# A z tile in pieces of the front stage, and a substitution moved from GpSimd to VectorE

## The reference, cut to what matters

```
proj = rmsnorm(x) @ w_in                 # 1024 -> xr, yr (512 each), qkv (1536), z (512), gates
h    = rglru(conv(xr)); out_rg = gelu(yr) * h          # gates: sigmoid(xc @ w_a), sigmoid(xc @ w_i)
q,k,v = silu(conv(qkv)); q, k normalized per head
per chunk of tokens and head: A = I + strict_lower(beta * (k k^T) * decay)
u, w = A^-1 [beta v, beta k e^g];  qk = (q k^T) * decay
S, o: recurrence over chunks from qk, u, w
out_gdn = rmsnorm(o) * silu(z)
x = x + [out_rg, out_gdn] @ w_out;  x = x + (silu(hf w_gate) * (hf w_up)) @ w_down
```

## Time and profile before

| | before |
|---|---|
| three runs | 1474.85, 1476.22, 1478.69 us; median 1476.22 |
| the profiled execution | 1474.63 us, span 1472.8 us |
| granted clock, mean | 0.985 |
| PE busy | 1416.4 us, 96% |
| DVE, ACT, POOL busy | 625.5, 373.3, 158.6 us |
| input block | 0 to 328.7 us |
| front stage | 328.7 to 400.8 us |
| sample states, two z tiles | 400.8 to 456 us |
| chunk loop begins | 462.1 us |

### The profile page before, as it was taken

One profiled execution on the slowest core, in us unless ns is written; L12 is line 12 of the kernel. 1 busy time (PEld: TensorE's weight loads), 2 busy tenths in 40 slices (PEclk: granted clock), 3 DMA queues, 4 the chain that ended last, 5 costly groups with the idle time before them and its releaser, 6 DMA issues.

```text
span 1472.8 us, 20785 instructions
## 1 busy us (share of the span) xinstructions
PE 1416.4 (96%) x8140; PEld 1299.6 (88%) x8140; DVE 625.5 (42%) x929; ACT 373.3 (25%) x612; POOL 158.6 (11%) x251
## 2 busy tenths in 40 slices
PE   6999999998898999999999999999999999999997
PEld 6888899997786899889898989898989898989895
DVE  6365455533352666643424242424242424242416
ACT  5345544332251222122020202020202020202012
POOL 3000000105474222210000000000000000000001
PEclk9999999997999999999999999999999999999999
DMA  6102211243544444327110101010101010100003
GB/s 224 62 18 75 75 69 74 100 145 133 194 173 126 140 129 126 123 99 283 54 58 29 57 28 57 28 57 28 57 28 57 28 57 28 57 28 28 0 0 121
DMA packets 66810, 119.93 MB, mean 81 GB/s; under 512 B 14672, under 2 KB 40208, under 8 KB 66768
## 3 DMA queue, kind: packets, MB, share of 16 engines
q1 hardware_dynamic: 66768, 119.36, 23.7%
HBM read 90.00 MB, written 29.34 MB: 81 GB/s over the span
## 4 chain that ended last, share of the span: by engine, by line
PE 46%; issue 2%; DMA 2%; ACT 2%; DVE 1%; SPq 0%; POOL 0%; ACTq 0%; DVEq 0%; POOLq 0%
PE bank L92 16%; PE bank L94 15%; PE bank L93 15%; ACT gu_hi L2060 1%; DMA gu_first_raw<-in_w_up 1%; DMA out_y<-y_out 1%; DVE acc L2146 0%; DVE y_out L2110 0%; DVE hf L2122 0%; ACT y_out L2096 0%; SPq L1987 0%; ACT gu_first_hi L2060 0%; SPq L1983 0%; POOL fstat L2161 0%; ACTq L81 0%
## 5 line engine op out<-in xcount | busy, mean ns | idle before, releaser
L92 PE MATMUL bank<-ht_hi,w_hi 128*128 128x364 f32 (+1 forms) x576 | 191.5, 332 | 0.0
L94 PE MATMUL bank<-ht_hi,w_lo 128*128 128x364 f32 (+1 forms) x576 | 189.9, 330 | 0.0
L93 PE MATMUL bank<-ht_lo,w_hi 128*128 128x364 f32 (+1 forms) x576 | 189.8, 330 | 0.0
L2122 DVE TENSOR_TENSOR hf<-sg,bank 128x364 f32<-128x364 f32 (+1 forms) x66 | 35.1, 532 | 338.6 <-PE bank L94 335.3
L92 PE MATMUL bank<-ht_hi,gu_hi 128*128 128x364 f32 (+1 forms) x528 | 173.2, 328 | 0.9 <-DVE hf L2122 0.9
L92 PE MATMUL bank<-ht_hi,gu_first_hi 128*128 128x364 f32 (+1 forms) x528 | 173.6, 329 | 0.5 <-PEq L930 0.5
L94 PE MATMUL bank<-ht_hi,gu_first_lo 128*128 128x364 f32 (+1 forms) x528 | 173.5, 329 | 0.0
L93 PE MATMUL bank<-ht_lo,gu_first_hi 128*128 128x364 f32 (+1 forms) x528 | 173.4, 328 | 0.0
L93 PE MATMUL bank<-ht_lo,gu_hi 128*128 128x364 f32 (+1 forms) x528 | 173.1, 328 | 0.0
L94 PE MATMUL bank<-ht_hi,gu_lo 128*128 128x364 f32 (+1 forms) x528 | 173.1, 328 | 0.0
L2146 DVE TENSOR_TENSOR acc<-acc,bank 128x512 f32<-128x512 f32 (+1 forms) x198 | 132.3, 685 | 90.3 <-PE bank L94 90.3
(11 more groups left out here) (297 smaller groups left out, 2213.5 us busy)
## 6 DMA issues: line engine op xcount, KB each, us to landing
w_raw<-in_w_in SPq DMA_DIRECT2D x24, 512.0 KB, 4.4
dn_raw<-in_w_down SPq DMA_DIRECT2D x22, 512.0 KB, 4.3
scratch_qkv<-cb_y SPq DMA_DIRECT2D x12, 512.0 KB, 2.7
scratch_kept<-kept SPq DMA_DIRECT2D x8, 768.0 KB, 3.7
gu_first_raw<-in_w_gate SPq DMA_DIRECT2D x11, 512.0 KB, 3.5
gu_first_raw<-in_w_up SPq DMA_DIRECT2D x11, 512.0 KB, 4.4
gu_raw<-in_w_gate SPq DMA_DIRECT2D x11, 512.0 KB, 3.5
gu_raw<-in_w_up SPq DMA_DIRECT2D x11, 512.0 KB, 4.4
```

Source lines behind the costliest of these rows:

```text
L92: pe.matmul(out, w_hi, x_hi, start=start, stop=False)
L93: pe.matmul(out, w_hi, x_lo, start=False, stop=False)
L94: return pe.matmul(out, w_lo, x_hi, start=False, stop=stop)
L2122: eng.tensor_tensor(hf[b][:, 0:m], sg[b][:, 0:m], psum[2 * b + 1][:, 0:m], ALU.mult).then_inc(hf_done, 1)
```

## The change

Three parts, with their edits. *The look-ahead in the RG-LRU loop:* the first token group of tile 2j+4 is projected ahead of the gate products of pass j, in all four passes; the next pass, or the qkv tiles after the loop, do groups 1 and 2 of that tile.

```diff
-            def project(t, s):
+            def project(t, s, groups=range(3)):
                 eng.wait_ge(w_hi_done, t + 1)
                 eng.wait_ge(w_lo_done, t + 1)
                 eng.wait_ge(evac_done, t)
...
             def rg_tile(j):
-                project(2 * j + 2, 0)
-                if isinstance(j, int) and j == 0:
+                first = isinstance(j, int) and j == 0
+                project(2 * j + 2, 0, range(0 if first else 1, 3))
+                if first:
                     turn_gates()
                 project(2 * j + 3, 1)
-                if isinstance(j, int) and j == 0:
+                project(2 * j + 4, 0, range(1))
+                if first:
                     eng.wait_ge(graw_done, 1)
...
-            with eng.Fori(1, PAIRS) as j:
-                two_tiles(TQ)(j)
-            two_tiles(TZ)(0)
+            project(TQ + 2, 0, range(1, 3))
+            project(TQ + 3, 1)
+            with eng.Fori(2, PAIRS) as j:
+                for s in range(2):
+                    project(TQ + 2 * j + s, s)
+            project(TZ, 0)
```

```diff
             for s in range(2):
-                load_w(TZ + s, s)
-            for s in range(2):
                 eng.wait_ge(cb_out[s], 16 * PAIRS)
             for c in range(3):
                 eng.dma_start(k["qk_b"][c][:, :, :], chunk_of(scratch["qkv"][0:2 * H], c)).then_inc(q_ld[c], 16)
             for s in range(2):
-                eng.wait_ge(evac_done, TZ + s + 2)
-                eng.dma_start(scratch["z"][s], cb_y[s][:, 0:SEQ]).then_inc(z_out[s], 16)
+                load_w(TZ + s, s)
+            eng.wait_ge(evac_done, TZ + 2)
+            eng.dma_start(scratch["z"][0], cb_y[0][:, 0:SEQ]).then_inc(z_out[0], 16)
             eng.wait_ge(st_out, 48)
...
+            def z1_step(n):
+
+                g, f = divmod(n, KT)
+                a, w = GROUPS[g]
+                if g and f == 0:
+                    eng.wait_ge(m_["z_ev"], g)
+                mm = mm3(eng, psum[7][:, 0:w], w_hi[1][:, f, :], w_lo[1][:, f, :],
+                         ht_hi[:, f, a:a + w], ht_lo[:, f, a:a + w], f == 0, f == KT - 1)
...
             for f in FRONTS:
                 nxt = FRONTS[f.a + 1] if f.a + 1 < MT else None
+                z1_some(1)
                 if nxt:
                     front(nxt)
+                z1_some(1)
                 turn_k(f)
                 if nxt:
                     decay(nxt)
+                z1_some(1)
                 products(f)
...
                 if f.a == 0:
-                    eng.wait_ge(w_in1, 16 * W_TILES // 2)
-                    eng.activation(w_hi[1][:, :, :], w_raw1[:, :, :], ACT.Copy).then_inc(w_hi_done, 1)
+                    split_w(0)
+                if f.a in (2, 4, 7):
+                    keep_z1((2, 4, 7).index(f.a))
+                if f.a == 7:
+                    eng.wait_ge(m_["z_mm"], 3)
+                    split_w(1)
...
-                if f.a > 2:
-                    eng.wait_ge(m_[f"kept_out{f.c % 2}"], 80 * (f.c // 2))
+                if f.a > 3:
+                    eng.wait_ge(m_[f"kept_out{f.c % 3}"], 80 * (f.c // 3))
...
             def chunk(c, s, nth, t, t2, more=True):
                 if not t.samples:
                     square_o(t)
+                    silu_z(t)
                 eng.wait_ge(m_["v_tr"], c + 1)
```

```diff
                 new_values(0)
-                for h in range(1, H):
-                    new_values(h)
-                    new_state(h - 1)
+                new_values(1)
+                new_state(0)
+                substitute(6)
+                new_values(2)
+                substitute(3)
+                new_state(1)
+                substitute(5)
+                new_values(3)
+                substitute(3)
+                new_state(2)
                 eng.wait_ge(m_["qs_mm"], H)
...
                 new_state(H - 1)
+                substitute(BLOCK)
...
+            def substitute(steps):
+
+                if n_sub[0] == 0:
+                    eng.wait_ge(m_["zeroed"], 7)
+                    eng.wait_ge(m_["sub_out"], 16)
+                for j in itertools.islice(columns, steps):
+                    rows, cols = BLOCK - 1 - j, j + 1
+                    part = sub_t[:, 0:rows * cols].rearrange("p (i k) -> p i k", k=cols)
+                    step(eng.tensor_tensor(part, sub_u[:, j, j + 1:].unsqueeze(2).to_broadcast([P, rows, cols]),
+                                           sub_x[:, j, 0:cols].unsqueeze(1).to_broadcast([P, rows, cols]), ALU.mult))
+                    below = sub_x[:, j + 1:, 0:cols]
+                    step(eng.tensor_tensor(below, below, part, ALU.subtract))
...
             for h in range(H):
                 eng.wait_ge(m_["samp_state"], h + 1)
                 eng.dma_start(o["S_sample"][h], s_states[h]).then_inc(m_["st_out"], 16)
+            eng.wait_ge(m_["sub_done"], 1)
+            eng.dma_start(scratch["sx"].rearrange("p (j i) -> p j i", i=BLOCK), sub_x[:, :, :]).then_inc(m_["sub_out"], 16)
             for f in range(3, 6):
                 load_wo(f)
```

More of the change, by code:

```diff
@@ L48 @@
 BANK = 512
-MID = 18
 XN = 3
@@ L387, in project @@
                 eng.wait_ge(evac_done, t)
-                for n, (a, m) in enumerate(GROUPS):
+                for n in groups:
+                    a, m = GROUPS[n]
                     for f in range(KT):
@@ L560, in _ @@
                 qkv(j)
[L562 to L570, removed]
+            eng.wait_ge(cb_out[0], 16 * PAIRS)
+            for n, (a, m) in enumerate(GROUPS):
+                e = min(a + m, SEQ)
+                eng.wait_ge(proj, 3 * TZ + n + 1)
+                eng.activation(cb_y[0][:, a:e], bank(0, n)[:, 0:e - a], ACT.Copy)
+            eng.activation(samp_z[:, 0, :], sample_bank(0), ACT.Copy).then_inc(evac_done, 1)
         @block.vector
@@ L809, in mixer_block @@
     kt2, e2, gr2 = ([four(f"{n}{s}") for s in range(2)] for n in ("kt", "decay", "gr"))
-    kept = [B(f"kept{s}", [P, 3 * H, P]) for s in range(2)]
-    s_kn, s_u, s_mq, s_v, s_kg, s_ktail, s_pp = (
-        four(n) for n in ("s_kn", "s_u", "s_mq", "s_v", "s_kg", "s_ktail", "s_pp"))
+    kept = [B(f"kept{s}", [P, 3 * H, P]) for s in range(3)]
+    s_kn, s_v, s_kg, s_ktail = (four(n) for n in ("s_kn", "s_v", "s_kg", "s_ktail"))
+    s_u, s_mq = (B(n, [P, H, TS]) for n in ("s_u", "s_mq"))
     assert B.at <= k["after_wo"]
@@ L863, in __init__, with kept_count @@
                 self.qkv = qk_b[self.c % 3]
-                self.kn, self.u, self.mq = (kept[self.c % 2][:, q * H:(q + 1) * H, :] for q in range(3))
+                self.kn, self.u, self.mq = (kept[self.c % 3][:, q * H:(q + 1) * H, :] for q in range(3))
                 self.tle, self.ugt = tle, ugt
+    def kept_count(q):
+        return 80 * len(range(q, NC, 3))
     FRONTS = [Front(a) for a in range(MT)]
@@ L933, in _ @@
         def _(eng):
-            for h, sem in ((0, "ss_ld0"), (1, "ss_ld1")):
-                eng.dma_start(s_states[h], i["state_S"][h]).then_inc(m_[sem], 16)
+            for h in range(2):
+                eng.dma_start(s_states[h], i["state_S"][h]).then_inc(m_["ss_ld0"], 16)
             def load_wo(f):
@@ L1200, in project_z, with z1_some @@
                     mm.then_inc(m_["z_mm"], 1)
+            def z1_step(n):
[5 more added lines that the diff above has]
+                         ht_hi[:, f, a:a + w], ht_lo[:, f, a:a + w], f == 0, f == KT - 1)
+                if f == KT - 1:
+                    mm.then_inc(m_["z_mm"], 1)
+            z1_steps = iter(range(3 * KT))
+            def z1_some(n):
+                for q in itertools.islice(z1_steps, n):
+                    z1_step(q)
             front(FRONTS[0])
@@ L1635, in samples_states, with step @@
                 new_state(H - 1)
+                substitute(BLOCK)
+            n_sub = [0]
+            def step(ins):
+                ins.then_inc(m_["sub_chain"], 1)
+                n_sub[0] += 1
+                eng.wait_ge(m_["sub_chain"], n_sub[0])
+            columns = iter(range(BLOCK - 1))
+            def substitute(steps):
[9 more added lines that the diff above has]
+                    step(eng.tensor_tensor(below, below, part, ALU.subtract))
+                    if j == BLOCK - 2:
+                        eng.memset(sub_t[:, 0:1], 0.0).then_inc(m_["sub_done"], 1)
             sums_of(FRONTS[0])
@@ L1695, in low_wo @@
                 if f == 0:
-                    eng.wait_ge(m_["kept_out1"], 80 * NC // 2)
+                    for q in range(3):
+                        eng.wait_ge(m_[f"kept_out{q}"], kept_count(q))
                 if f >= 6:
```

155 lines of the change are left out of this document (79 added, 76 removed).

## The result

The changed kernel takes 1498.39 us (median of 4 runs, 1497.58 to 1499.37), the kernel before beside it 1476.7: a ratio of 1.0147, 95% interval 1.0129 to 1.0165. It is slower by 1.5%, as forecast in sign; 1491 was forecast, with a range of 1483 to 1499, and the measured time lies at its upper end (21.7 us slower where 16.3 was forecast). The profiled execution took 1498.99 us, its span is 1497.2, 24.4 more than before's 1472.8.

A forecast was written before the change was run, and what follows sets the result against it. TensorE, busy 96% of the span, was taken as the bound, with changes only where it waits or runs at 1.2 GHz. Terms 13.9 - 5.7 + 3.2 + 4.4 + 0.5 = +16.3 us gave 1491 us, range 1483 to 1499.

The forecast's parts named there:

- The loop: RG-LRU loop: early group waits for late weights, 8.3 us, plus 5.6 us of low clock: +13.9 us.
- Rival 2: RG-LRU loop: low-part weights arrive within 19.8 us, the group fills the wait, loop -9 us, time 1468; chance 0.12.
- The block's end: End of input block: a tile of 11.8 us goes, but SyncE's queue delays the front stage: -5.7 us.
- The front stage: Front stage: added pieces 6 us, ScalarE's copies 3.4, less 6 from the clock: +3.2 us, bounds -5 and +9.
- in return the denser products should bring the clock back earlier than after 17.0 us: Front stage start: denser products shorten the half-clock stretch, winning 6 of at most 8.5 us.
- the two places where ScalarE holds up the next front: Front stage: copy behind the fourth sample-free front, and the last with the fourth tile's split; 1.7 us each, 3.4 together.
- the third buffer removes that wait: Front stage: a third kept buffer ends the normalized keys' wait for the store, gaining 0.86 us in seven passes.
- Rival 4: Front stage: the third kept buffer gains nothing, stage +9 us, time 1497; chance included in the forecast's 0.62.
- The substitution: Sample states to first chunk: VectorE's 23.2 us delays the norm, 7.4 us stand at the turn; +4.4 us in all.
- Rival 3: Substitution: broadcast operands cost VectorE double, 46 us, stand at the turn grows 10 to 15, time 1503; chance 0.11.
- The chunk loop: Chunk loop: Silu adds one ScalarE instruction of some 0.6 us per chunk, mostly hidden: +0.5 us in all.
- Rival 1: Whole kernel: added pieces keep TensorE busy enough that no stand brings 1.2 GHz, sum +1.6, 1476 to 1478; chance 0.15.

The follow-up runs named there:

- the early load alone: Kernel before plus the early token group, with SyncE's weight loads moved ahead of the recurrence's store, VectorE's order unchanged: 1485.85 us, ratio 1.0055.
- the run without the group: Changed kernel with the early token group taken out, RG-LRU loop and qkv tiles as before, all else as changed: 1481.45 us, ratio 1.0030.
- the last two runs: Changed kernel with early loads and low part, ScalarE's tasks later, block-end loads behind the meeting: 1466.3 us (substitution on VectorE, norm between its columns), 1463.15 us (on GpSimd).
- the early group alone: Kernel before with only the early token group of the RG-LRU loop added: 1494.08 us, ratio 1.0107.
- the run with both moves: Kernel before plus the early group, SyncE's loads ahead of the store wait and VectorE's low part ahead of the convolution: 1469.67 us, ratio 0.9950.

## Why the prediction was right, and where it was not

*The loop: right, by its mechanism and its size.* Forecast were a stand of 4.2 us, passes of 32.2 us and 1.3 us of clock; the stands are 3.15 to 4.25 us, the passes 33.6, 34.1 and 34.4 us with the clock in them, and the sum is the forecast's +13.9. That it agrees so closely is partly luck: from gates to gates the three later passes came out 1.6 us longer in all than forecast, the first pass 0.4 shorter, and 1.1 us came back behind the loop, where before had 3.4 us at 1.2 GHz and the changed kernel has none. The clock was put a little low: all four stands were followed by 3.4 us at 1.2 GHz, the upper bound of 6.8 us. By the rule of "TensorE: Matmul & The Clock Gate", section "HAM oscillation — how this bites in real kernels", in the Trainium skill (a loop that waits for a transfer in every pass falls to the low clock in every pass) the term would have been that bound, and the changed kernel agrees. Not every run does: with the substitution on GpSimd, whose loop is the same, the stand of 3.31 us in the second pass was followed by 2.4 GHz, and so were the stands of 2.5 to 2.7 us with the early load alone. Rival 2 had its condition right: with the low part there in time the loop gives -7.4 us, against -9 by its sum.

*The block's end: right.* SyncE's z store leaves at 334.45, 5 us after TensorE's last product; some 7 were said, and the term came out at -7.3, not -5.7, within its bounds.

*The front stage: wrong, beyond its bounds.* The step "in return the denser products should bring the clock back earlier than after 17.0 us: of the 8.5 us that this costs at most I take 6" failed: the stretch is 17.1 us. And the two places where ScalarE holds up the next front, put at 1.7 us each for the stand, had stands of 1.56 and 0.91 us, and 6.8 us at 1.2 GHz followed each. Within the stage half-clock time is 28.3 us against 23.9: 2.2 us lost where 6 were to be won. Of the two places one was named rightly (the copy behind the fourth front); the second stand (0.91 us) came from the samples' first spread, which was there before, not from the split of the fourth tile. The pass itself came out as summed, 7.61 us against 7.62, for a wrong reason: "the third buffer removes that wait" is not what took the 0.86 us away; the pieces fill it with two buffers as well. Rival 4 was right about the buffers and wrong about the pass.

*The substitution: right in every step but the clock.* Its pieces took 3.51, 2.30, 4.37, 2.70 and 10.25 us, against 3.5, 2.35, 4.4, 2.75 and 10.2; the third z product is 3.2 us late (3.1 said); the stand at the turn is 6.44 us (7.4 said), and there is none ahead of the first chunk. But 10.2 us at 1.2 GHz came with it. The first 3.6 of them lie in the stand itself, and in the rest TensorE was busy for 6.56 us: a cost of at most 3.3 us, not the 5.1 that two of the expectations take. With 3.4 us at 1.2 GHz around the start of the third z product (445.5), in which TensorE was busy throughout, that is 5.0 where 1.7 was taken. Rival 3 (VectorE dear) fell: the 62 instructions with broadcast operands took 23.1 us, against 23.2 reckoned from plain ones.

*The chunk loop:* +1.0 for 0.5, within what runs that leave this part alone differ by (1006.3 to 1009.5).

The sum of the terms missed by 8 us of span, nearly all of it the clock of the front stage; what the block's end gave beyond its term (1.6) and the turn cost beyond its own (1.5) cancel. So the time came out in its range with one term far out. Rival 1 (the clock holds) is the opposite of what happened.

## What to carry to other kernels

Work put ahead of a wait to fill it must have its own inputs by then: follow each back through every queue it passes, and count from the event that closes the loop. One queue entry (here a load behind a store) and one place in a vector queue decided between +17 and -7 us for the same products. Work moved to a faster engine is judged by what is queued behind it: here a stand went from the chunk to the turn, to the output weights and back to the chunk, and the slower, idle engine was no worse.

## What the runs showed of the hardware

The clock follows stands unevenly. In the changed kernel each stand in the loop (3.15 to 4.25 us) was followed by 3.4 us at 1.2 GHz. In the run with the substitution on GpSimd, whose loop is the same, one was not; its timeline and its table of stretches:

```profile
120.94 0.41 PE L91 MATMUL bank<-ht_hi,w_hi 128*128 128x364 f32 x1 [3.31 <-issue]
...
120.90:124.30 3.40, 3.36 (x20) 3.39 (x21) 1.16 (x1) 2.21 (x5) 0.00 (x0) 1.00 0.00 0
```

Stands of 2.5 to 2.7 us with the early load alone were not followed by it either. The one of 2.02 us in the earlier trace rows was, but the same stand ahead of the same products was not in the run without the group:

```profile
86.58 4.59 PE L407 MATMUL bank<-rb_xc,rg_w 128*128 128x372 f32 x12 [2.02 <-issue]
...
88.00:91.40 3.40, 3.33 (x12) 1.77 (x12) 0.76 (x1) 2.53 (x6) 0.00 (x0) 1.00 0.00 0
```

In the front stage the clock fell behind 6.8 us in which TensorE was busy all the time, and with the same code there it fell, behind the stage's start, once in one of the last two runs and not at all in the other. What decides stays open.

And the same code of the front stage took 72.0 us in the kernel before, 72.4 and 78.3 in the runs with the early load alone and the early group alone, and 81.8 in the profile of the run with both moves. Nothing in the stage was changed. The time at 1.2 GHz in it was 23.9, 23.9, 37.5 and 41.0 us, and half of the extra time makes up most of the difference. A single profile is no measure of that stage.
